# Stationary operands at byte 64, moving operands at byte 0 of each 128 bytes

## The chip, the cores and the metric

The kernel runs on one core of a Trainium2 chip. The core has TensorE (PE: matmuls; PEld: its weight loads), VectorE (DVE), ScalarE (ACT), GpSimd (POOL) and SyncE (SP, which only issues DMAs here), with SBUF and PSUM as on-chip memories of 128 partitions. The metric is the device time of one execution in microseconds (us); lower is better. Before the change three runs gave 1592.0 us as median (1591.66 to 1597.04).

## The reference

Two transformer blocks run one after the other on 256 tokens of width 1024, each two layers deep, all in float32.

```python
# first block, per layer: x and ctx are 256 tokens each; ctx is updated in layer 0 alone
sh1, sc1, gt1, sh2, sc2, gt2 = split(silu(c) @ w_ada + b_ada, 6)     # and the same for ctx
px = (rms_norm(x, g1) * (1 + sc1) + sh1) @ w_in
mix = concat([attention(q, k, v), fourier_mix(f), spatial_gate(u, gv)]) @ w_out
x = x + gt1 * mix
x = x + gt2 * (square(relu(modulate(rms_norm(x, g2)) @ w1)) @ w2)    # w1: 1024 x 4096
# second block, per layer
proj = rms_norm(x, g) @ w_in                                         # 1024 x 3656
x = x + concat([moba(...), diff_attention(...), sparse_attention(...)]) @ w_out
x = x + (silu(h @ w_gate) * (h @ w_up)) @ w_down                     # 1024 x 2816 and back
```

Nearly all the arithmetic is in the products with the large weights.

## The kernel before

**Three products for one.** A product of two float32 matrices is made of three matmuls of the type fp32r. Each operand is split into a high part and the rest, and hi x hi, hi x lo and lo x hi are summed in PSUM (`three`, line 2218; its matmul is line 2220). A matmul has a *stationary* operand (128 columns, loaded into the array by a LDWEIGHTS) and a *moving* one, which streams through. The load for the next matmul runs beside the stream of the present one. In the trace a matmul reads `output<-moving,stationary`.

**Which operand is which.** Where rows of tokens are the output (`rows1`, `rows2`, `down`), the activations are stationary (`act_hi`, `act_lo`, `hid1_*`, `hid2_*`, 128 tokens each) and 512 columns of weights move (256 or 328 in two blocks of the second `w_in`). Where columns are the output (`up1`, `up2`), 128 columns of weights are stationary and 512 tokens move in layer 0 of the first block, 256 tokens elsewhere. The opening of the first `up1` (`up1_open`) takes the two streams apart and so moves 256.

**Where weights come from.** SP loads 512 KB pieces into a ring of eight slots, `raw`; ScalarE writes the high part to `w_hi` (line 1175), VectorE the rest to `w_lo` (line 1581); TensorE multiplies, which frees the slot. `raw_of`, `hi_of` and `lo_of` give a piece's place; each slot has 32 floats (128 bytes) more than it needs, and `begins` (line 644) says at which float in the slot the piece starts: 16 (byte 64) for the kind "narrow", 0 for others. "narrow" are the up-products' weights with 256 moving columns, of `up1` in layer 1 and of `up2`.

**Where activations come from.** The norms and the mixing stages write `act_hi` on ScalarE and `act_lo` on VectorE. The same two tensors are stationary in `rows1`, `rows2` and `down` (through `act_of`) and moving in `up1`, `up2`.

**Order.** Every engine's program is written out by hand: `program` walks through the stages, and the tables FILL, FILL2 and OUT2 name the steps that are put between the weight pieces: turns (transposes on TensorE: data stationary, the identity moving), scores, values, modulation products. Buffers of stages that are not alive together share addresses, each following on the one before it, so a tensor's byte modulo 128 follows from the sizes ahead of it; `pad` shifts it.

Of the kernel before, what the change touches and what calls it, by code (L numbers as in the profile page):

```python
# [14 lines left out]
P = 128  # L15
# [87 lines left out]
def build(nc, A, consts, out, n):  # L103
    top = ExitStack()
    with top:
# [10 lines left out]
        act_hi = sb("act_hi", [P, KT, 2 * NT], F32R)  # L116
        act_lo = sb("act_lo", [P, KT, 2 * NT], F32R)
# [28 lines left out]
        with ExitStack() as s:  # L146
            cond_raw = sb("cond_raw", [P, KT, 2], F32, s)
            cond = sb("cond", [P, KT, 32], F32, s)
            mod = sb("mod", [P, 48, 2], F32, s)
# [3 lines left out]
            gains1 = sb("gains1", [P, DEPTH, 2 * DH + 256], F32, s)  # L153
            w_sp = sb("w_sp", [P, 4, P], F32, s)
            b_sp = sb("b_sp", [P, DEPTH, 4], F32, s)
            pad("pad_b_sp", 96, s)
            mod_rows = sb("mod_rows", [P, 2, W], F32, s)
            gate_b = sb("gate_b", [P, 2, D], F32, s)
# [4 lines left out]
            with ExitStack() as s2:  # L163
                proj1 = sb("proj1", [P, 2 * TT, IN1], F32, s2)
                q_t = sb("q_t", [P, NQ1 // 2, 2 * NT], F32, s2)
                k_t = sb("k_t", [P, NKV1, 2 * NT], F32, s2)
                four = sb("four", [P, 2, 2 * NT], F32, s2)
                w_sp_t = sb("w_sp_t", [P, 4, P], F32, s2)
                gtmp = sb("gtmp", [P, TT, 512], F32, s2)
# [4 lines left out]
                with ExitStack() as s3:  # L174
                    kdup = sb("kdup", [P, 2 * TT, 2 * NKV1, DH], F32, s3)
                with ExitStack() as s3:
                    probs1 = sb("probs1", [P, 2, 2, 2 * NT], F32, s3)
                    probs_t1 = sb("probs_t1", [P, 2, 2, 2 * TT, P], F32, s3)
# [4 lines left out]
            with ExitStack() as s2:  # L183
                xn1 = sb("xn1", [P, 2 * TT, D], F32, s2)
                below_wide = sb("below_wide", [P, 2 * TT, D], F32, s2)
                wide = sb("wide", [P, 4, NT], F32, s2)
        with ExitStack() as s:
# [5 lines left out]
            with ExitStack() as s2:  # L193
                proj2 = sb("proj2", [P, TT, IN2], F32, s2)
                pad("pad_proj2", 64, s2)
                pairs_t = sb("pairs_t", [P, 21, NT], F32, s2)
                ikdup = sb("ikdup", [P, TT, 2, DH], F32, s2)
                seen = sb("seen", [P, TT, NT], BF16, s2)
                relu_t = sb("relu_t", [P, 2, 2 * NT], F32, s2)
                score = sb("score", [P, TT, NT], F32, s2)  # L200
                diff_rows = sb("diff_rows", [P, TT, 4 * P], F32, s2)
                lam_in = diff_rows[:, :, 0:4 * DH]
# [3 lines left out]
                rope_a2 = sb("rope_a2", [P, 2, 512], F32, s2)  # L206
                probs2 = sb("probs2", [P, 2, 2, NT], F32, s2)
                probs_t2 = sb("probs_t2", [P, 4, 2 * TT, P], F32, s2)
            with ExitStack() as s2:
                hid2_hi = sb("hid2_hi", [P, FF2 // P, NT], F32R, s2)  # L210
                hid2_lo = sb("hid2_lo", [P, FF2 // P, NT], F32R, s2)
                fa2 = sb("fa2", [P, 2, 2 * NT], F32, s2)
                fb2 = sb("fb2", [P, 2, 2 * NT], F32, s2)
                xn_beside = sb("xn_beside", [P, TT, D], F32, s2)
            with ExitStack() as s2:
                xn2 = sb("xn2", [P, TT, D], F32, s2)
# [427 lines left out]
        def begins(i):  # L644

            return 16 if i < len(n.slots) and n.slots[i][0] == "narrow" else 0
# [221 lines left out]
        class Sync(Phases):  # L868
# [66 lines left out]
            def up1(self, l, h):  # L935
# [19 lines left out]
            def up2(self, l):  # L955
                for j in range(FF2 // 256):
                    for w in ("w_gate_2", "w_up_2"):
                        src = A[w][l].rearrange("(k p) n -> p k n", p=P)
                        for q in range(2):
                            self.put("narrow", 1024, lambda r: [(tiles(r, 4), src[:, 4 * q:4 * q + 4, j * 256:(j + 1) * 256])])  # L960
# [195 lines left out]
        class Scalar(Splitting):  # L1156
# [61 lines left out]
            def norm_part(self, m, which, streams, k0, k1):  # L1218
# [3 lines left out]
                for k in range(k0, k1):  # L1222
# [7 lines left out]
                    for s in streams:  # L1230
                        wait_wide(self.e, m, s, k)
                        nc.scalar.copy(act_hi[:, k, s * NT:(s + 1) * NT], wide_at(m, s, k)).then_inc(norm_hi, 1)
                        n.put("norm_hi", (m, s, k))

            def context_part(self, m, which, k0, k1):

                for k in range(k0, k1, 2):
# [8 lines left out]
                    nc.scalar.copy(act_hi[:, k:k + 2, 0:NT], wide[:, k % 4:k % 4 + 2, :]).then_inc(norm_hi, 1)  # L1246
# [16 lines left out]
            def norm_high(self, m, t, a):  # L1263
                self.e.wait_ge(xn_turned, n.at("xn_turned", (m, t, a)))
                nc.scalar.copy(act_hi[:, 4 * a:4 * a + 4, NT + t * P:NT + (t + 1) * P], tiles(turned_bank(m, t, a)[:], 4)).then_inc(norm_hi, 1)
# [132 lines left out]
            def out_(self, st, j):  # L1398
# [4 lines left out]
                nc.scalar.copy(act_hi[:, k:k + 2, c:c + NT], tiles(bank[b][:], 2)).then_inc(mix_hi, 1)  # L1403
# [50 lines left out]
            def diff_turn(self, l, t):  # L1454
                self.e.wait_ge(mix_full, n.at("mix_full", ("diff", l, t)))
                nc.scalar.mul(act_hi[:, 2 + 2 * t:4 + 2 * t, 0:NT], tiles(bank[7][:], 2), sub_g[:, l:l + 1]).then_inc(mix_hi, 1)
# [113 lines left out]
        class Vector(Splitting):  # L1570
# [90 lines left out]
            def context_part(self, m, k0, k1, row=None):  # L1661
# [4 lines left out]
                def low(k):  # L1666
                    e.wait_ge(norm_hi, n.at("norm_hi", (m, CTX, k + 1)))
                    nc.vector.tensor_tensor(act_lo[:, k:k + 2, 0:NT], wide[:, k % 4:k % 4 + 2, :], act_hi[:, k:k + 2, 0:NT].bitcast(F32),
# [17 lines left out]
            def norm_part(self, m, streams, k0, k1):  # L1686
# [4 lines left out]
                def low(k):  # L1691
                    for s in streams:
                        e.wait_ge(norm_hi, n.at("norm_hi", (m, s, k)))
                        nc.vector.tensor_tensor(act_lo[:, k, s * NT:(s + 1) * NT], wide_at(m, s, k),
                                                act_hi[:, k, s * NT:(s + 1) * NT].bitcast(F32), ALU.subtract).then_inc(norm_lo, 1)
# [46 lines left out]
            def norm_low(self, m, t, a):  # L1742
                self.e.wait_ge(norm_hi, n.at("norm_hi", (m, t, a)))
                at_ = slice(4 * a, 4 * a + 4), slice(NT + t * P, NT + (t + 1) * P)
                nc.vector.tensor_tensor(act_lo[:, at_[0], at_[1]], tiles(turned_bank(m, t, a)[:], 4), act_hi[:, at_[0], at_[1]].bitcast(F32),  # L1745
# [180 lines left out]
            def mix_low(self, key, b, k, c):  # L1926
                self.e.wait_ge(mix_hi, n.at("mix_hi", key))
                nc.vector.tensor_tensor(act_lo[:, k:k + 2, c:c + NT], tiles(b, 2), act_hi[:, k:k + 2, c:c + NT].bitcast(F32),
# [149 lines left out]
            def diff_turn(self, l, t):  # L2078
                self.e.wait_ge(mix_hi, n.at("mix_hi", ("diff", l, t)))
                c = slice(2 + 2 * t, 4 + 2 * t)  # L2080
                nc.vector.scalar_tensor_tensor(act_lo[:, c, 0:NT], tiles(bank[7][:], 2), sub_g[:, l:l + 1], act_hi[:, c, 0:NT].bitcast(F32),
# [135 lines left out]
        class Tensor(Phases):  # L2217
# [141 lines left out]
            def act_of(self, k, g):  # L2359
                return [a[:, k, g * P:(g + 1) * P] for a in (act_hi, act_lo)]  # L2360
# [333 lines left out]
            def up1_open(self):  # L2694

                e, m, first = self.e, 1, self.i
                for s in (CTX, X):
                    for j in range(2):
# [3 lines left out]
                        for q in range(2):  # L2702
# [9 lines left out]
                            for kk, f in ((kk, f) for kk in range(4) for f in range(2)):  # L2712
                                k, idx = 4 * q + kk, 2 * j + f
                                if j == f == 0:
                                    e.wait_ge(norm_lo, n.at("norm_lo", (m, s, k)))
                                ins = self.three(up1_bank(0, 0, idx)[:, s * NT:(s + 1) * NT], [v[:, kk, f * P:(f + 1) * P] for v in w],
                                                 [a[:, k, s * NT:(s + 1) * NT] for a in (act_hi, act_lo)], (s, k) == (CTX, 0))
# [6 lines left out]
            def up1(self, l, h):  # L2724
# [8 lines left out]
                for j in range(opened, FF1 // 256 // HALVES[l]):  # L2733
                    for q in range(2):
# [4 lines left out]
                        for f in range(2):  # L2739
# [6 lines left out]
                            for kk in range(4):  # L2746
# [3 lines left out]
                                ins = self.three(o, [v[:, kk, f * P:(f + 1) * P] for v in w], [a[:, k, c0:2 * NT] for a in (act_hi, act_lo)],  # L2750
# [140 lines left out]
```

## Time and profile before

| | |
|---|---|
| median of three runs | 1592.0 us |
| profiled execution | 1594.35 us, span 1592.6 us |
| TensorE busy | 97% of the span, 9164 matmul records |
| weight loads | 79% |
| VectorE, ScalarE, GpSimd | 65%, 50%, 7% |
| DMA | 202 GB/s on average, 322 MB |

The span is the time from the first to the last instruction of the profiled execution. Matmuls overlap: a record with 512 columns lasts some 392 ns, but the next one starts before it ends, so busy time says little and the distance between starts says much. A float32 matmul that isn't a turn has two records, a three-product matmul and a turn have one. The up-products of the second block (1076 to 1196 us and 1409 to 1528 us) are the "narrow" ones. The trace is of one execution, and line numbers are those of the kernel before.

### The profile page before, as it was taken

How to read it: one execution, taken by the hardware profiler on the slowest of the kernel's cores; microseconds unless marked ns; L12 is line 12 of the kernel's file. 1: busy time of each engine (PE TensorE's matmuls, PEld its weight loads, DVE VectorE, ACT ScalarE, POOL GpSimd, SP SyncE). 2: the span in 40 equal slices, each digit the busy share in tenths (PEclk: the TensorE clock that was granted, in tenths of full speed). 3: DMA queues.
4: the chain of work that ended last, by engine and by line, in shares of the span. 5: the costliest groups of instructions: out<-in, count | busy, mean ns of one | idle time of the engine just before them, and what ended most of it. 6: DMA issues, size and time to landing. Idle time of an engine off the chain costs nothing.

```text
span 1592.6 us, 23486 instructions
## 1 busy us (share of the span) xinstructions
PE 1541.2 (97%) x9164; PEld 1262.6 (79%) x9164; DVE 1028.4 (65%) x1577; ACT 795.5 (50%) x1356; POOL 114.2 (7%) x130
## 2 busy tenths in 40 slices
PE   6999999999999999998999999999999999999999
PEld 2864689778888887567898878779998787689987
DVE  3637756455456437576785576978995558879973
ACT  3537735343345225565664456645554456555542
POOL 0111000010001000100000031010000111000000
PEclk9999999999999999999999999999999999999999
DMA  9528623487568524586998689436665596356653
GB/s 360 152 84 313 215 75 114 145 264 253 162 220 277 162 66 133 176 279 190 335 319 300 211 272 312 160 108 183 191 197 191 184 326 227 106 141 192 198 190 115
DMA packets 201005, 322.41 MB, mean 202 GB/s; under 512 B 14576, under 2 KB 100864, under 8 KB 200768
## 3 DMA queue, kind: packets, MB, share of 16 engines
q1 hardware_dynamic: 192992, 293.51, 57.6%
q0 software_dynamic: 7680, 27.34, 4.8%
q8 instruction: 73, 1.20, 0.3%
q14 instruction: 36, 0.29, 0.1%
q10 hardware_dynamic: 224, 0.07, 0.0%
HBM read 298.27 MB, written 22.61 MB: 201 GB/s over the span
## 4 chain that ended last, share of the span: by engine, by line
PE 86%; DVE 7%; DMA 3%; ACT 2%; issue 1%; POOL 0%; SPq 0%; POOLq 0%; DVEq 0%; ACTq 0%
PE bank L2220 53%; PE pair_bank L2220 21%; PE bank L2289 2%; DVE w_lo L1581 1%; PE bank L2537 1%; PE pair_bank L2506 1%; DMA raw<-in_w_in 1%; PE bank L2517 1%; DMA raw<-in_w_ada 1%; PE bank L2315 1%; PE pair_bank L2557 1%; DMA raw<-in_w_mlp 1%; PE bank L2425 0%; PE bank L2571 0%; ACT w_hi L1175 0%
## 5 line engine op out<-in xcount | busy, mean ns | idle before, releaser
L1581 DVE TENSOR_TENSOR w_lo<-raw,w_hi 128x1024 fp32r<-128x1024 f32 (+2 forms) x374 | 447.4, 1218 | 273.5 <-ACT w_hi L1175 272.0
L1175 ACT CAST w_hi<-raw 128x1024 fp32r<-128x1024 f32 (+1 forms) x416 | 428.4, 1045 | 363.2 <-PE bank L2220 236.6
L2220 PE MATMUL pair_bank<-act_hi,w_hi 128*128 128x256 f32 (+1 forms) x744 | 226.8, 305 | 5.0 <-DVE act_lo L1745 2.1
L2220 PE MATMUL pair_bank<-act_hi,w_lo 128*128 128x256 f32 (+1 forms) x744 | 224.7, 302 | 0.0
L2220 PE MATMUL pair_bank<-act_lo,w_hi 128*128 128x256 f32 (+1 forms) x744 | 224.6, 302 | 0.0
L2220 PE MATMUL bank<-w_hi,hid_hi 128*128 128x512 f32 x560 | 220.2, 393 | 0.0
L2220 PE MATMUL bank<-w_lo,hid_hi 128*128 128x512 f32 x560 | 219.6, 392 | 0.0
L2220 PE MATMUL bank<-w_hi,hid_lo 128*128 128x512 f32 x560 | 219.4, 392 | 0.0
L2220 PE MATMUL bank<-w_hi,act_hi 128*128 128x512 f32 (+2 forms) x528 | 206.6, 391 | 8.4 <-DVE w_lo L1581 4.0
L2220 PE MATMUL bank<-w_hi,act_lo 128*128 128x512 f32 (+2 forms) x528 | 200.3, 379 | 0.0
L2220 PE MATMUL bank<-w_lo,act_hi 128*128 128x512 f32 (+2 forms) x528 | 200.1, 379 | 0.0
L2220 PEld LDWEIGHTS pair_bank<-act_hi,w_hi 128*128 128x128 f32 x744 | 140.9, 189 | 16.6 <-issue 6.4
L2220 PE MATMUL bank<-act_hi,w_hi 128*128 128x256 f32 (+1 forms) x504 | 148.7, 295 | 0.9 <-DVE w_lo L1581 0.9
L2220 PE MATMUL bank<-act_hi,w_lo 128*128 128x256 f32 (+1 forms) x504 | 147.9, 293 | 0.0
L2220 PE MATMUL bank<-act_lo,w_hi 128*128 128x256 f32 (+1 forms) x504 | 147.8, 293 | 0.0
L2220 PEld LDWEIGHTS pair_bank<-act_lo,w_hi 128*128 128x128 f32 x744 | 140.8, 189 | 7.2 <-issue 0.7
L2220 PEld LDWEIGHTS pair_bank<-act_hi,w_lo 128*128 128x128 f32 x744 | 140.7, 189 | 6.3
L2220 PEld LDWEIGHTS bank<-w_hi,hid_hi 128*128 128x128 f32 x560 | 105.1, 188 | 23.9 <-issue 0.2
L2220 PEld LDWEIGHTS bank<-w_hi,hid_lo 128*128 128x128 f32 x560 | 105.1, 188 | 23.9
L2220 PEld LDWEIGHTS bank<-w_lo,hid_hi 128*128 128x128 f32 x560 | 105.2, 188 | 23.6 <-issue 0.2
L2220 PEld LDWEIGHTS bank<-w_hi,act_hi 128*128 128x128 f32 x528 | 100.0, 189 | 29.1 <-DVE w_lo L1581 5.3
L2220 PEld LDWEIGHTS bank<-w_hi,act_lo 128*128 128x128 f32 x528 | 99.9, 189 | 19.3
(249 smaller groups left out, 2088.9 us busy)
## 6 DMA issues: line engine op xcount, KB each, us to landing
raw<-in_w_mlp SPq DMA_DIRECT2D x128, 512.0 KB, 4.9
raw<-in_w_in SPq DMA_DIRECT2D x112, 512.0 KB, 4.5
raw<-in_w_ada SPq DMA_DIRECT2D x96, 512.0 KB, 5.6
raw<-in_w_gate SPq DMA_DIRECT2D x44, 512.0 KB, 3.8
raw<-in_w_up SPq DMA_DIRECT2D x44, 512.0 KB, 3.8
raw<-in_w_down SPq DMA_DIRECT2D x44, 512.0 KB, 3.6
split_lo<-w_lo POOLq DMA_DIRECT2D x36, 512.0 KB, 5.0
w_lo<-split_lo SPq DMA_DIRECT2D x36, 512.0 KB, 5.1
```

What stands on the lines that cost most here:

```text
L1175: nc.scalar.copy(hi_of(i)[:, 0:w], raw_of(i)[:, 0:w]).then_inc(hi_ready, 1)
L1581: nc.vector.tensor_tensor(lo_of(i)[:, 0:w], raw_of(i)[:, 0:w], hi_of(i)[:, 0:w].bitcast(F32), ALU.subtract).then_inc(lo_ready, 1)
L2220: ins = nc.tensor.matmul(o, a[x], b[y], start=first and i == 0, stop=True, skip_group_check=True)
L2289: ins = nc.tensor.matmul(bank[bk][j:j + 32, :], cond[:, k, :], tiles(raw[:, r, 0:1024], 2)[:, kk, :], start=k < 4, stop=True, skip_group_c ...
L2315: nc.tensor.matmul(bank[bk][:], sel_b[:, s, :], mod_rows[:, bk % 2, :], start=True, stop=True, skip_group_check=True).then_inc(ada_turned, 1)
L2506: nc.tensor.matmul(bank[a][:, 0:w], st["q"][a], st["k"][a], start=True, stop=True).then_inc(scored, 1)
L2517: ins = nc.tensor.matmul(st["o"][a], st["v"][a][kt], probs_t1[:, j % 2, a, kt, :], start=kt == 0, stop=kt == keys - 1)
L2537: ins = nc.tensor.transpose(bank[2 + a][:, kt * P:(kt + 1) * P], probs1[:, j % 2, a, kt * P:(kt + 1) * P], ident)
L2557: nc.tensor.matmul(bank[a][:, 0:w], st["q"][a], st["k"][a], start=True, stop=False)
```

## The change

The change moves operands within 128 bytes and does nothing else: instructions, their order and their waits are the same on every engine. Pads of 64 bytes are put into the SBUF allocation; the kind "narrow" is named "up" and now holds layer 0 of `up1` too; and `act_hi`, `act_lo` get rows of 512 + 32 floats with two views of the same memory, one that starts at byte 64 (index 0, for uses as stationary) and one at byte 0 (index 1, for uses as moving). Norms write the view that the next product reads (`m % 2` is 1 ahead of the up-products).

Bytes modulo 128 of the operands, from the allocation:

| matmuls | count | stationary, moving before | after |
|---|---|---|---|
| three products, 512 columns | 3840 | 0, 0 | 64, 0 |
| three products, 256 columns, `up1` layer 1 and `up2` | 2880 | 64, 0 | 64, 0 |
| three products, 256 columns, others (192 in `up1_open`) | 336 | 0, 0 | 64, 0 |
| three products, 328 columns | 96 | 0, and 0, 32 or 64 | 64, and 0, 32 or 64 |
| turns of activations, probabilities and modulation rows | 632 | 0 (40 at 32), 0 | 64 (40 at 96), 0 |
| scores and values of the first block | 208 | 0, 0 | 64, 0 |
| values of the second block with stationary `proj2` | 48 | 0 or 32, and 0 or 8 | 64 or 96, the same |
| modulation (`ada`) | 192 | 0, 0 | 64, 0 |
| scores and logits of the second block, mask products | 160 | 0, 0 | 0, 0 |
| values of the second block with moving `proj2` | 24 | 0, and 0 or 32 | 0, and 64 or 96 |
| Fourier, spatial and gate products | 54 | 0 or 8, and 0, 8 or 124 | 64 or 8, and 0, 8, 64 or 124 |

```diff
-        act_hi = sb("act_hi", [P, KT, 2 * NT], F32R)
-        act_lo = sb("act_lo", [P, KT, 2 * NT], F32R)
+        act_hi_room = sb("act_hi_room", [P, KT, 2 * NT + 32], F32R)
+        act_lo_room = sb("act_lo_room", [P, KT, 2 * NT + 32], F32R)
+
+        def act_views(room):
+            return [room[:, :, at_:at_ + 2 * NT] for at_ in (16, 0)]
+
+        act_hi, act_lo = act_views(act_hi_room), act_views(act_lo_room)
...
             cond_raw = sb("cond_raw", [P, KT, 2], F32, s)
+            pad("pad_cond", 64, s)
             cond = sb("cond", [P, KT, 32], F32, s)
+            pad("end_cond", 64, s)
...
+                pad("pad_proj1", 64, s2)
                 proj1 = sb("proj1", [P, 2 * TT, IN1], F32, s2)
                 q_t = sb("q_t", [P, NQ1 // 2, 2 * NT], F32, s2)
+                pad("end_q_t", 64, s2)
                 k_t = sb("k_t", [P, NKV1, 2 * NT], F32, s2)
...
+                pad("pad_hid1", 64, s2)
                 hid1_hi = sb("hid1_hi", [P, 16 * 2 * NT], F32R, s2)
                 hid1_lo = sb("hid1_lo", [P, 16 * 2 * NT], F32R, s2)
+                pad("pad_fa1", 64, s2)
...
+                pad("pad_hid2", 64, s2)
                 hid2_hi = sb("hid2_hi", [P, FF2 // P, NT], F32R, s2)
                 hid2_lo = sb("hid2_lo", [P, FF2 // P, NT], F32R, s2)
+                pad("pad_fa2", 64, s2)
...
-            return 16 if i < len(n.slots) and n.slots[i][0] == "narrow" else 0
+            return 16 if i < len(n.slots) and n.slots[i][0] == "up" else 0
...
-                        self.put("narrow" if l else "w", 1024, lambda r: [(tiles(r, 4), src[:, 4 * q:4 * q + 4, c:c + 256])])
+                        self.put("up", 1024, lambda r: [(tiles(r, 4), src[:, 4 * q:4 * q + 4, c:c + 256])])
...
-                        nc.scalar.copy(act_hi[:, k, s * NT:(s + 1) * NT], wide_at(m, s, k)).then_inc(norm_hi, 1)
+                        nc.scalar.copy(act_hi[m % 2][:, k, s * NT:(s + 1) * NT], wide_at(m, s, k)).then_inc(norm_hi, 1)
...
-                nc.scalar.copy(act_hi[:, k:k + 2, c:c + NT], tiles(b, 2)).then_inc(mix_hi, 1)
+                nc.scalar.copy(act_hi[0][:, k:k + 2, c:c + NT], tiles(b, 2)).then_inc(mix_hi, 1)
...
-                return [a[:, k, g * P:(g + 1) * P] for a in (act_hi, act_lo)]
+                return [a[:, k, g * P:(g + 1) * P] for a in (act_hi[0], act_lo[0])]
...
-                                ins = self.three(o, [v[:, kk, f * P:(f + 1) * P] for v in w], [a[:, k, c0:2 * NT] for a in (act_hi, act_lo)],
+                                ins = self.three(o, [v[:, kk, f * P:(f + 1) * P] for v in w], [a[:, k, c0:2 * NT] for a in (act_hi[1], act_lo[1])],
...
```

The lines left out are pads of the same kind (around `w_sp`, `mod_rows`, `w_sp_t`, `kdup`, `probs1`, `xn1`, `wide`, `proj2`, `ikdup`, `diff_rows`, `probs2`, `xn_beside`, `xn2`) and the same two indices at the other places that write or read `act_hi` and `act_lo`.

## Rows read from the trace of the kernel before

**Rows 1.** The page, parts 1 and 2: the span, busy times, TensorE's clock.

```profile
span 1592.6 us, 23486 instructions
...
PE 1541.2 (97%) x9164; PEld 1262.6 (79%) x9164; DVE 1028.4 (65%) x1577; ACT 795.5 (50%) x1356; POOL 114.2 (7%) x130
...
PEclk9999999999999999999999999999999999999999
```

**Rows 2.** TensorE's waits: who waited for whom, us in total, times, longest.

```profile
PE bank L2289 <- DMA raw<-in_w_ada: 5.1, 1, 5.1
...
PE bank L2220 <- DVE w_lo L1581: 4.8, 5, 2.1
```

**Rows 3.** Windows, line 2220 alone: stretch, length, PE busy (starts), clock, DMA share, GB/s.

```profile
45.40:98.60 53.20, 52.57 (x228) 1.00 0.39 112
192.00:229.00 37.00, 37.00 (x162) 1.00 0.19 58
262.40:335.40 73.00, 68.55 (x290) 1.00 0.52 168
336.00:604.00 268.00, 266.31 (x1152) 1.00 0.59 193
703.00:725.00 22.00, 21.95 (x95) 1.00 0.64 199
832.90:920.90 88.00, 88.00 (x385) 1.00 0.77 250
1196.00:1256.50 60.50, 60.50 (x265) 1.00 0.57 178
1528.50:1589.00 60.50, 60.50 (x265) 1.00 0.43 141
```

**Rows 4.** Chain that ended last: start us, length us, engine, output, line, matmuls.

```profile
237.92 5.76 PE pair_bank L2220 x48
...
1076.17 11.24 PE pair_bank L2220 x96
1087.40 10.88 PE bank L2220 x96
```

**Rows 5.** Windows, line 2220 alone, three short stretches.

```profile
381.44:387.79 6.35, 6.35 (x29) 1.00 0.35 90
429.68:435.29 5.61, 5.61 (x25) 1.00 0.52 180
1076.10:1079.70 3.60, 3.53 (x30) 1.00 0.33 119
```

**Rows 6.** TensorE's timeline, 328 columns: seventh and tenth matmul after a turn.

```profile
962.58 0.31 PE L2220 MATMUL bank<-w_hi,act_hi 128*128 128x328 f32 x1
...
963.03 0.31 PE L2220 MATMUL bank<-w_hi,act_hi 128*128 128x328 f32 x1
```

**Rows 7.** Chain that ended last: turns of both blocks.

```profile
44.96 0.44 PE pair_bank L2338 x4
...
961.41 0.44 PE bank L2425 x4
```

**Rows 8.** Windows, all engines: length, busy us (instructions) each, clock, DMA share, GB/s.

```profile
104.00:188.00 84.00, 80.41 (x596) 44.43 (x594) 57.54 (x155) 61.75 (x163) 7.98 (x5) 0.96 0.73 260
216.00:600.00 384.00, 384.00 (x1789) 313.70 (x1788) 197.69 (x244) 150.38 (x205) 20.20 (x37) 1.00 0.54 176
1073.00:1187.00 114.00, 112.24 (x988) 111.79 (x987) 103.27 (x85) 59.07 (x73) 0.59 (x1) 1.00 0.64 186
```

**Rows 9.** The page, part 5: the split of the weights; us busy, mean ns.

```profile
L1581 DVE TENSOR_TENSOR w_lo<-raw,w_hi 128x1024 fp32r<-128x1024 f32 (+2 forms) x374 | 447.4, 1218 | 273.5 <-ACT w_hi L1175 272.0
L1175 ACT CAST w_hi<-raw 128x1024 fp32r<-128x1024 f32 (+1 forms) x416 | 428.4, 1045 | 363.2 <-PE bank L2220 236.6
```

**Rows 10.** Windows, all engines, projections of the second block, both layers.

```profile
924.00:1019.00 95.00, 92.12 (x486) 71.99 (x485) 67.85 (x162) 57.04 (x127) 22.75 (x19) 1.00 0.84 277
1282.00:1320.00 38.00, 38.00 (x210) 31.45 (x209) 20.95 (x55) 24.21 (x59) 5.68 (x4) 1.00 0.97 320
```

More of the change, by code:

```diff
@@ L153, in build @@
             gains1 = sb("gains1", [P, DEPTH, 2 * DH + 256], F32, s)
+            pad("pad_w_sp", 64, s)
             w_sp = sb("w_sp", [P, 4, P], F32, s)
@@ L157, in build @@
             mod_rows = sb("mod_rows", [P, 2, W], F32, s)
+            pad("end_mod_rows", 64, s)
             gate_b = sb("gate_b", [P, 2, D], F32, s)
@@ L163, in build @@
             with ExitStack() as s2:
+                pad("pad_proj1", 64, s2)
                 proj1 = sb("proj1", [P, 2 * TT, IN1], F32, s2)
                 q_t = sb("q_t", [P, NQ1 // 2, 2 * NT], F32, s2)
+                pad("end_q_t", 64, s2)
                 k_t = sb("k_t", [P, NKV1, 2 * NT], F32, s2)
                 four = sb("four", [P, 2, 2 * NT], F32, s2)
+                pad("pad_w_sp_t", 64, s2)
                 w_sp_t = sb("w_sp_t", [P, 4, P], F32, s2)
+                pad("end_w_sp_t", 64, s2)
                 gtmp = sb("gtmp", [P, TT, 512], F32, s2)
@@ L174, in build @@
                 with ExitStack() as s3:
+                    pad("pad_kdup", 64, s3)
                     kdup = sb("kdup", [P, 2 * TT, 2 * NKV1, DH], F32, s3)
                 with ExitStack() as s3:
+                    pad("pad_probs1", 64, s3)
                     probs1 = sb("probs1", [P, 2, 2, 2 * NT], F32, s3)
+                    pad("end_probs1", 64, s3)
                     probs_t1 = sb("probs_t1", [P, 2, 2, 2 * TT, P], F32, s3)
             with ExitStack() as s2:
+                pad("pad_hid1", 64, s2)
                 hid1_hi = sb("hid1_hi", [P, 16 * 2 * NT], F32R, s2)
                 hid1_lo = sb("hid1_lo", [P, 16 * 2 * NT], F32R, s2)
+                pad("pad_fa1", 64, s2)
                 fa1 = sb("fa1", [P, 2, 2 * NT], F32, s2)
             with ExitStack() as s2:
+                pad("pad_xn1", 64, s2)
                 xn1 = sb("xn1", [P, 2 * TT, D], F32, s2)
                 below_wide = sb("below_wide", [P, 2 * TT, D], F32, s2)
+                pad("pad_wide", 64, s2)
                 wide = sb("wide", [P, 4, NT], F32, s2)
@@ L193, in build @@
             with ExitStack() as s2:
+                pad("pad_proj2", 64, s2)
                 proj2 = sb("proj2", [P, TT, IN2], F32, s2)
-                pad("pad_proj2", 64, s2)
                 pairs_t = sb("pairs_t", [P, 21, NT], F32, s2)
+                pad("pad_ikdup", 64, s2)
                 ikdup = sb("ikdup", [P, TT, 2, DH], F32, s2)
+                pad("end_ikdup", 64, s2)
                 seen = sb("seen", [P, TT, NT], BF16, s2)
@@ L200, in build @@
                 score = sb("score", [P, TT, NT], F32, s2)
+                pad("pad_diff_rows", 64, s2)
                 diff_rows = sb("diff_rows", [P, TT, 4 * P], F32, s2)
+                pad("end_diff_rows", 64, s2)
                 lam_in = diff_rows[:, :, 0:4 * DH]
@@ L206, in build @@
                 rope_a2 = sb("rope_a2", [P, 2, 512], F32, s2)
+                pad("pad_probs2", 64, s2)
                 probs2 = sb("probs2", [P, 2, 2, NT], F32, s2)
+                pad("end_probs2", 64, s2)
                 probs_t2 = sb("probs_t2", [P, 4, 2 * TT, P], F32, s2)
             with ExitStack() as s2:
+                pad("pad_hid2", 64, s2)
                 hid2_hi = sb("hid2_hi", [P, FF2 // P, NT], F32R, s2)
                 hid2_lo = sb("hid2_lo", [P, FF2 // P, NT], F32R, s2)
+                pad("pad_fa2", 64, s2)
                 fa2 = sb("fa2", [P, 2, 2 * NT], F32, s2)
                 fb2 = sb("fb2", [P, 2, 2 * NT], F32, s2)
+                pad("pad_xn_beside", 64, s2)
                 xn_beside = sb("xn_beside", [P, TT, D], F32, s2)
             with ExitStack() as s2:
+                pad("pad_xn2", 64, s2)
                 xn2 = sb("xn2", [P, TT, D], F32, s2)
@@ L2716, in up1_open @@
                                 ins = self.three(up1_bank(0, 0, idx)[:, s * NT:(s + 1) * NT], [v[:, kk, f * P:(f + 1) * P] for v in w],
-                                                 [a[:, k, s * NT:(s + 1) * NT] for a in (act_hi, act_lo)], (s, k) == (CTX, 0))
+                                                 [a[:, k, s * NT:(s + 1) * NT] for a in (act_hi[1], act_lo[1])], (s, k) == (CTX, 0))
                                 if s == X and k == KT - 1 and f == 0:
@@ L2848, in up2 @@
                                     ins = self.three(b[:, f * NT:(f + 1) * NT], [v[:, kk, f * P:(f + 1) * P] for v in w],
-                                                     [a[:, k, NT:2 * NT] for a in (act_hi, act_lo)], k == 0 and f == 0)
+                                                     [a[:, k, NT:2 * NT] for a in (act_hi[1], act_lo[1])], k == 0 and f == 0)
                             self.took(ins, ("up2", l, j, which) if q == 1 else None)
```

22 lines of the change are left out of this document (11 added, 11 removed).

## The prediction

> **What bounds the kernel now.** I read the page's first two parts first. TensorE is busy for 97% of the span, VectorE for 65%, and TensorE's clock is granted at 9 tenths or more in every slice [rows 1]. Then the waits of TensorE: the longest is the first load, and those for the split of the weights come to 4.8 us in five waits [rows 2]. So nearly everything that ends late is TensorE's own work. Then I asked the windows and the chain of waits for the *pace*: they give a time and a count of back-to-back matmuls, and time over count is the distance from one matmul's start to the next. That distance, not the duration of one matmul (which overlaps its successor), is what the end of the kernel is made of. Of the three-product matmuls 3840 have 512 moving columns, 3216 have 256 and 96 have 328. In eight stretches 2842 of the 512-column ones keep TensorE busy for 655.4 us, 230.6 ns each [rows 3]: 41% of the span in one kind of instruction. DMA moves 58 to 250 GB/s there. The other 998 or so stand in short groups between turns, scores and values.
>
> **What the placement does to the pace.** The kernel already holds both placements for one shape. The opening products of the first MLP have 256 columns with stationary and moving both at byte 0: 48 in 5.76 us, 120.0 ns each. The later up-products have 256 columns too, with the stationary at byte 64: 96 in 10.88 us, 113.3 ns each [rows 4]. The difference is 6.7 ns. What a column costs comes from two shapes in the same placement: the steadiest 512-column stretch has 29 starts, 28 intervals, in 6.35 us, 226.7 ns [rows 5] against 120.0 for 256, so 0.417 ns per column, one column per cycle at 2.4 GHz, the level that the clock share of 1.00 in those rows means. The fixed part is then 120.0 - 106.7 = 13.3 ns with both at byte 0, and 6.7 ns with the stationary at 64. If it depends on the length as little with 64 as it does with 0, a settled 512-column matmul takes 213.3 + 6.7 = 220.0 ns.
>
> Two things speak for caution. First, 64 alone doesn't give the low pace: it settles. The first 96 of a run of up-products take 11.24 us, the next 96 take 10.88 [rows 4], and the first 30 go by in 3.53 us, 118 ns each [rows 5]. Second, the 328-column products read moving operands at bytes 0, 32 and 64 in turn against a stationary at byte 0. Those at 64, which lie as far apart as the change wants it, take 0.45 us for three, 150 ns [rows 6]; 328 x 0.417 + 13.3 is 150.0. They gain nothing. They are groups of three, so they may never settle; or longer products don't profit at all. That is the main doubt.
>
> **The change part by part.**
> - *Long runs of 512 columns.* 2842 x (230.6 - 220.0) = 30.1 us. Until a run settles it stays near its old pace. Modulation and gate products cut the eight stretches into some 15 runs; 15 x 12 matmuls x 10 ns = 1.8 us less, so 28.3 us. Bounds: at the top, all of the fixed part goes, 2842 x (230.6 - 213.3) = 49 us; at the bottom, the pace becomes that of the worst steady stretch of today, 24 intervals in 5.61 us, 233.8 ns [rows 5], which loses 2842 x 3.2 = 9 us. I take 220.0, as the nearest shape (same operands, same loads) shows it.
> - *Short groups of 512, and 328.* About 1000 and 96 matmuls, mostly in groups of 9 to 24 that are cut by turns. By the 328s they gain nothing; by the unsettled up-products, 118 against 120, 2 ns each, 2 us in all. I take 1 us. At the bottom they lose the same 3.2 ns, 3 us.
> - *Opening products.* 192 of 256 columns go from 120.0 to 113.3: 1.3 us; with settling I take 1.0.
> - *Turns.* Their stationary moves from byte 0 (in one tensor every other one at 32) to 64 (96). Four take 0.44 us, 110 ns each, whether all stand at byte 0 (line 2338) or two at 0 and two at 32 (line 2425, second block) [rows 7]. So I take 0; if the 632 of them moved as the products do, by 6.7 ns, it would be 4 us either way, mostly where TensorE waits in any case.
> - *Scores, values and modulation.* In the attention of the first layer, 596 matmul records, weights are being loaded for only 44 of 84 us, and ScalarE is busy for 62 and VectorE for 58 [rows 8]: loads lie much less beside streams there. I take 0; the bound by 6.7 ns a record is 4 us either way, and as much for the two layers' other attention stretches together.
> - *VectorE, ScalarE, DMA.* Instructions, order and waits are the same; only addresses differ. What hides their work is TensorE's pace: in the two-row stages 512 KB of weights feed 12 matmuls, 2.77 us now, 2.64 afterwards. The split of such a piece takes 1.05 us on ScalarE and 1.22 us on VectorE [rows 9], so both stay below. The loads rise from 178 to some 187 GB/s in the last stage and from 250 to 262 in the fullest of rows 3, which is below what the projections of the second block draw, 277 and 320 GB/s [rows 10]. If that cover went, a stretch would fall back to its loads; only those projections are near it, and I book 0.5 us lost there.
>
> Sum: 28.3 + 1 + 1 - 0.5 = 30 us. The profiled execution took 1594.35 us (span 1592.6 and 1.75 around it), so 1564.4 for one like it; the median of the runs shown is 2.35 us below it, so 1562.
>
> The Trainium skill has a rule against this: SBUF — State Buffer, table of the section "A bandwidth-pool intuition that's wrong (but worth ruling out)", gives TensorE a second independent read port for loading weights, beside that for the moving operand. By that the placement is nothing and the time stays 1592. The 120.0 against 113.3 ns of one shape does not fit the rule; the 328 columns do [rows 4, 6]. Its page TensorE: Matmul & The Clock Gate, section "Back-to-back issue gap", gives N/2.4 + 2.5 ns for a warm matmul, 215.8 ns for 512 columns; the stretches of rows 3 are 15 ns above it, and by it the first term would be 42 us.
>
> **Rivals.**
> 1. *Longer products don't profit* (no change, 1591). In the up stage TensorE is loading weights for 111.8 of 114 us; in the first layer's MLP, nearly all of 512 columns, for 314 of 384 [rows 8]. So a load that is disturbed less shortens the first, and in the second it has time to spare. For it: the 328 columns. Against it: the fixed part is 13.3 ns at 256, 328 and 512 columns alike with both at 0, as if one cause made it. Only the opening products gain then, 1 us.
> 2. *It settles halfway* (1580). 226.7 ns is a steady state that exists today [rows 5]. If 64 only makes all long runs reach it, the term is 2842 x 3.9 = 11 us, and 1 for the rest: 1592 - 12.
> 3. *It settles wrongly* (slower, 1602). The same kernel has steady stretches at 233.8 ns with its operands at byte 0 like all others [rows 5], so the place within 128 bytes isn't all that counts. If the pairs at 64 fall into that state in the long runs, it costs 9 us, and 1 in the short groups. It decides from a pace above 230.6.
> 4. *More than I booked* (about 1548): the fixed part falls to half of 6.7 ns, 9.5 us more, and the short groups settle too, 1000 x 5 ns.
>
> **How the numbers follow.** My forecast, long runs settled near 220 ns, has a chance of 0.50 and by itself a range of 1555 to 1573 (settling in a few or in many matmuls). Rival 1: 0.17. Rival 2: 0.16. Rival 3: 0.09. Rival 4: 0.08. A difference under 0.5%, 8 us, can't be told from none here. So faster: 0.50 + 0.16 + 0.08 = 0.74; same: rival 1 and a little of rival 3, 0.18; slower: 0.08. The range, 1552 to 1591, takes in rivals 1 and 2 and leaves out rival 3 and most of rival 4.
>
> **What would show it.** The two windows of 60.5 us with 265 matmuls shrink to 58, the 88 us with 385 to 84.5. The opening 48 take 5.5 us. The up-products keep 113.3 ns and four turns 0.44 us. TensorE's waits stay within a few us. If the 512-column pace is 230 with the rest as said, rival 1 is right; 226.7 or 234 would be rivals 2 and 3. If the pace is 220 and the end is still near 1590, the time went back to loads, which would stand in TensorE's waits as w_lo or raw.

## The result, and the profile after

The changed kernel takes 1604.0 us (median of four runs, 1602.6 to 1608.6) against 1592.3 for the kernel before beside it: a ratio of 1.0065, with a 95% interval of 1.0049 to 1.0081. It is slower by 0.65%, and the interval leaves out 1. The forecast was 1562 (1552 to 1591). The profiled execution took 1603.83 us, 9.5 more than that of before. Among all the runs below one stands apart and is left out of the ratios: of e5's six executions one took 3070.7 us, the others 1600.0 to 1602.4.

The page of the kernel after, parts 1 and 2, answers to [rows 1]:

```profile
span 1602.0 us, 23486 instructions
...
PE 1553.4 (97%) x9164; PEld 1272.4 (79%) x9164; DVE 1029.5 (64%) x1577; ACT 795.4 (50%) x1356; POOL 113.5 (7%) x130
...
PEclk8999999999999999999999999999999999999999
```

The same instructions ran, and VectorE, ScalarE and GpSimd were as busy as before. TensorE is busy for 12.2 us longer. In the first 40 us its granted clock is 0.87 of full speed after and 0.91 before; in all the windows below it is 1.00 in both. Its waits, the two of [rows 2] again (who waited for whom, us in total, times, longest):

```profile
PE bank L2319 <- DMA raw<-in_w_ada: 5.1, 1, 5.1
PE bank L2250 <- DVE w_lo L1611: 4.6, 4, 2.1
```

They are nearly what they were (5.1 and 4.8). So the time went into the distance between matmuls. Windows of the kernel after over the three-product line (2250 now) alone, in the columns of [rows 3]: stretch, length, PE busy (records), PEld busy (records), clock, DMA share, GB/s.

```profile
262.40:335.20 72.80, 68.35 (x289) 53.77 (x288) 1.00 0.52 168
335.90:424.90 89.00, 88.97 (x384) 72.16 (x384) 1.00 0.70 231
...
834.30:922.90 88.60, 88.60 (x385) 71.98 (x384) 1.00 0.76 249
...
1081.00:1191.00 110.00, 110.00 (x942) 110.00 (x941) 1.00 0.64 187
1201.20:1261.80 60.60, 60.60 (x265) 49.38 (x264) 1.00 0.56 177
...
1421.00:1531.00 110.00, 110.00 (x942) 110.00 (x941) 1.00 0.65 188
1537.80:1598.40 60.60, 60.60 (x265) 49.38 (x264) 1.00 0.43 140
```

The 512-column stretches are nearly where they were: the two of 265 take 60.60 us for 60.50, the one of 385 takes 88.60 for 88.00 [rows 3]. The new thing stands in the two windows of 110 us, which lie inside the up stages of the second block, 256 columns. Inside the same stages the kernel before has, with the same columns:

```profile
1080.00:1190.00 110.00, 110.00 (x973) 110.00 (x972) 1.00 0.66 193
...
1415.00:1525.00 110.00, 110.00 (x973) 110.00 (x972) 1.00 0.66 193
```

973 records fitted into 110 us, and now 942 do. (A count takes in two or three matmuls that began ahead of the window; by the distance of starts it is 113.3 ns before and 117.1 now.) The chain of waits shows it from the stage's first matmul on (start us, length us, engine, output, line, matmuls), against 11.24 and then 10.88 for 96 in [rows 4]; ahead of it stand the first opening products, 5.76 before, and four turns, 0.44 in [rows 7]:

```profile
44.78 0.44 PE pair_bank L2368 x4
...
238.30 5.60 PE pair_bank L2250 x48
...
1077.51 11.46 PE pair_bank L2250 x96
1088.97 11.24 PE bank L2250 x96
1100.21 11.24 PE pair_bank L2250 x96
```

The run of up-products never comes down to the low pace: it stays at 11.24 for 96, 117.1 ns each, where it had gone down to 10.88. The whole stages, 1056 products each, grow from 119.6 to 123.5 and 123.6 us, 7.9 us together; the up stage of the first block's layer 1 has 692 records in the 88 us from 739 on where it had 700, about 1 us. That is 8.9 of the 9.5 us. The opening products give back 0.16 us in the first 48 and 0.4 in all four groups; the eight 512-column stretches of [rows 3] lose 1.7 together, from first start to last; what lies between them gains about 0.7.

Yet the change leaves the up-products' bytes modulo 128 alone (64 and 0, before and after). What it alters for them is the *row* of their moving operand: a row of `act_hi` and `act_lo` was 2048 bytes and is now 2176, so that two k-tiles (blocks of 128 rows of the product's inner dimension) lie 2176 apart, and the low half lies 17408 bytes behind the high one in place of 16384.

### The profile page after: what moved, and what is told of

The parts are those of the page before. It is cut to its first block, busy times and chain, and to the rows that moved or that the text cites. A ratio compares the mean times of both kernels' runs of the same rounds, so it can differ in the third digit from the quotient of the medians.

```text
span 1602.0 us, 23486 instructions
## 1 busy us (share of the span) xinstructions
PE 1553.4 (97%) x9164; PEld 1272.4 (79%) x9164; DVE 1029.5 (64%) x1577; ACT 795.4 (50%) x1356; POOL 113.5 (7%) x130
## 4 chain that ended last, share of the span: by engine, by line
PE 86%; DVE 7%; DMA 2%; ACT 2%; issue 2%; POOL 0%; SPq 0%; POOLq 0%; DVEq 0%; ACTq 0%
PE bank L2250 53%; PE pair_bank L2250 21%; PE bank L2319 2%; DVE w_lo L1611 1%; PE bank L2567 1%; PE pair_bank L2536 1%; PE bank L2547 1%; DMA raw<-in_w_in 1%; PE bank L2345 1%; PE pair_bank L2587 1%; DMA raw<-in_w_ada 1%; DMA raw<-in_w_mlp 1%; PE bank L2455 0%; PE bank L2601 0%; ACT w_hi L1205 0%
## 5 line engine op out<-in xcount | busy, mean ns | idle before, releaser
L2250 PE MATMUL pair_bank<-act_hi_room,w_hi 128*128 128x256 f32 (+1 forms) x744 | 228.4, 307 | 3.8 <-DVE act_lo_room L1775 2.1
L2250 PE MATMUL pair_bank<-act_lo_room,w_hi 128*128 128x256 f32 (+1 forms) x744 | 226.2, 304 | 0.0
L2250 PE MATMUL pair_bank<-act_hi_room,w_lo 128*128 128x256 f32 (+1 forms) x744 | 225.9, 304 | 0.0
L2250 PE MATMUL bank<-w_hi,act_hi_room 128*128 128x512 f32 (+2 forms) x528 | 207.2, 393 | 7.5 <-DVE w_lo L1611 4.0
L2250 PE MATMUL bank<-w_hi,act_lo_room 128*128 128x512 f32 (+2 forms) x528 | 201.1, 381 | 0.0
L2250 PE MATMUL bank<-w_lo,act_hi_room 128*128 128x512 f32 (+2 forms) x528 | 200.5, 380 | 0.0
L2250 PEld LDWEIGHTS pair_bank<-act_hi_room,w_hi 128*128 128x128 f32 x744 | 140.8, 189 | 15.1 <-issue 6.0
L2250 PE MATMUL bank<-act_hi_room,w_hi 128*128 128x256 f32 (+1 forms) x504 | 150.0, 298 | 0.6 <-DVE w_lo L1611 0.6
L2250 PE MATMUL bank<-act_lo_room,w_hi 128*128 128x256 f32 (+1 forms) x504 | 149.1, 296 | 0.0
L2250 PE MATMUL bank<-act_hi_room,w_lo 128*128 128x256 f32 (+1 forms) x504 | 148.9, 295 | 0.0
L2250 PEld LDWEIGHTS bank<-w_hi,act_hi_room 128*128 128x128 f32 x528 | 100.1, 190 | 28.3 <-DVE w_lo L1611 5.3
```

The source lines that it names most:

```text
L2250: ins = nc.tensor.matmul(o, a[x], b[y], start=first and i == 0, stop=True, skip_group_check=True)
```

## The experiments

*Distance* below is the start of the stationary operand minus that of the moving one, in bytes modulo 256. *Pace* is the mean distance of successive starts, in the kernels of their own over the second half of a stretch.

### Which part of the change costs the time

Theory "row step": the up-products' 113.3 ns needs the moving rows to step by a multiple of 256 bytes. Rivals: the distance of the two halves ("low half"), or anything else in the change ("elsewhere"). The kernel before with the longer rows alone, the kernel after with the old rows, and the kernel after with rows of 2304 bytes:

```diff
# e1_rows2176, in the kernel before
-        act_hi = sb("act_hi", [P, KT, 2 * NT], F32R)
-        act_lo = sb("act_lo", [P, KT, 2 * NT], F32R)
+        act_hi_room = sb("act_hi_room", [P, KT, 2 * NT + 32], F32R)
+        act_lo_room = sb("act_lo_room", [P, KT, 2 * NT + 32], F32R)
+        act_hi, act_lo = act_hi_room[:, :, 0:2 * NT], act_lo_room[:, :, 0:2 * NT]
# e2_after_rows2048, in the kernel after (act_lo_room alike)
-        act_hi_room = sb("act_hi_room", [P, KT, 2 * NT + 32], F32R)
+        act_hi_room = sb("act_hi_room", [P, KT, 2 * NT], F32R)
-            return [room[:, :, at_:at_ + 2 * NT] for at_ in (16, 0)]
+            return [room[:, :, at_:at_ + 2 * NT] for at_ in (0, 0)]
# e3_after_rows2304, in the kernel after (act_lo_room alike)
-        act_hi_room = sb("act_hi_room", [P, KT, 2 * NT + 32], F32R)
+        act_hi_room = sb("act_hi_room", [P, KT, 2 * NT + 64], F32R)
```

Expected of the first:

> The kernel before, with nothing but the rows of act_hi and act_lo lengthened from 2048 to 2176 bytes (views still at byte 0 of the room, slots, pads and hidden tensors as before). 'Row step' and 'low half': up2 falls from 113.3 to 117 ns, the stage of 119.7 us takes 123.5, the kernel 1600 to 1606 us. 'Elsewhere': 1591 to 1594 us.

Of the second:

> The kernel after, with the rows of act_hi and act_lo back at 2048 bytes and both views at byte 0; everything else of the change stays. 'Row step' and 'low half': up2 back at 113.3 ns and 119.7 us, the kernel 1591 to 1595 us. 'Elsewhere': 1602 to 1606 us.

Of the third:

> The kernel after, with rows of 2304 bytes in place of 2176 (the views stay at byte 64 and byte 0). 'Row step' with a modulus of 256 bytes: up2 back at 113.3 ns, the kernel 1591 to 1595 us. 'Row step' with a larger modulus (512 and more), or 'low half' (18432 apart now), or 'elsewhere': 117 ns and 1602 to 1606 us.

Measured, beside 1594.2 us for the kernel before on that chip: e1 1603.6, ratio 1.0047 (1.0029 to 1.0066); e2 1595.5, 1.0001 (0.9986 to 1.0017); e3 1595.8, 1.0015 (0.9998 to 1.0032). One 110 us window in the first of the two up stages of e1, e2 and e3, three-product line alone:

```profile
1081.00:1191.00 110.00, 110.00 (x942) 110.00 (x941) 1.00 0.65 187
```

```profile
1078.00:1188.00 110.00, 110.00 (x973) 110.00 (x972) 1.00 0.66 193
```

```profile
1081.00:1191.00 110.00, 110.00 (x973) 110.00 (x972) 1.00 0.66 194
```

The longer row alone makes the kernel before slow, and taking it away, or giving it 128 bytes more, brings the 973 records back. "Elsewhere" falls; "low half" stands badly, since e3 moves the low half further still (18432). e2 and e3 end 0.5 and 0.8 us above the range that was expected of them, on a chip on which the kernel before took 1594.2. e3 says one thing more: it is the whole change with another row length, and it comes to nothing, 0.15% with an interval of -0.02% to 0.32%. (e2 takes back more than the rows: the stationary views of the two tensors start at byte 0 again.)

### The placements by themselves

A kernel without anything beside the products shows the paces one by one.

```python
# m1_places: one stretch; chain() yields byte places as the up-products walk them
for st, mv, b, first in chain(256, 96, sa=64, ma=1152, pitch=2048, apart=16384, slot=4224):
    nc.tensor.matmul(bank[b][:, 0:256], arena[:, st:st + P], arena[:, mv:mv + 256], start=first, stop=True, ...)
```

> A kernel of its own that leaves the whole computation out: 38 stretches of chained three-product sequences from one SBUF array, 288 products of 256 columns or 144 of 512 (180 of 384) each, two products of 512 and four of 64 columns between stretches; only the byte places differ. Stretch 1 has the places of the up-products of before (weights at byte 64 mod 128, slots 4224 bytes apart, moving rows 2048 bytes apart, low half 16384 bytes behind the high one), stretch 2 those of after (rows 2176 apart, low half 17408 behind). Theory 'row step' (the settled pace needs the moving row to keep its place modulo 256 bytes from one k to the next): stretch 1 at 113.3 ns, 2 and 3 (2176 apart) at 116 to 118, 4 (2048 apart, only the low half moved by 1024) at 113.3, 5 to 7 (2304, 2560, 3072 apart) at 113.3, 8 and 9 (2112, 2080 apart) above 115. Rival 'low half' (the distance of the two halves decides): 4 at 116 to 118 and 3 at 113.3. Rival 'elsewhere' (not the moving operand at all): 1 to 9 alike. Weights' start (stretches 10 to 16): 64 at 113.3, 0 at 119 to 120 if the opening products' pace comes from the place. 512 columns (stretches 26 to 36): 229 to 233 at every place if the placement in 128 bytes does not matter to them; one of them at 220 if the change only missed the right place.

Windows of m1_places over TensorE's matmuls, 15 us each, in the second half of stretches 1, 2, 4, 5, 8, 10 and 33: stretch, length, PE busy (records), clock, DMA share, GB/s.

```profile
64.00:79.00 15.00, 15.00 (x135) 1.00 0.00 1
99.00:114.00 15.00, 15.00 (x131) 1.00 0.00 1
168.00:183.00 15.00, 15.00 (x135) 1.00 0.00 1
201.00:216.00 15.00, 15.00 (x135) 1.00 0.00 1
302.00:317.00 15.00, 15.00 (x130) 1.00 0.00 1
372.00:387.00 15.00, 15.00 (x128) 1.00 0.00 1
...
1168.00:1183.00 15.00, 15.00 (x68) 1.00 0.00 1
```

| 256 columns, weights at byte 64, slots 4224 apart | pace, ns |
|---|---|
| rows 2048 apart, low half 16384 or 17408 behind | 113.3, 113.3 |
| rows 2176 apart, low half 17408 or 18432 behind | 116.3, 116.3 |
| rows 2304, 2560, 3072 apart | 113.3, 113.3, 113.3 |
| rows 2112, 2080 apart | 117.8, 118.0 |
| rows 2048 apart, weights at byte 0, 16, 32, 48, 80, 96, 112 | 117.7 to 118.9 |
| rows 2048 apart, moving rows at byte 32, 64, 64 of 128 | 118.8 to 119.0 |

"Row step" holds and "low half" falls: 17408 costs nothing with rows of 2048. (All distances of the halves tried here are multiples of 256 bytes.) For 256 columns the place within 128 bytes does matter, too: of the starts in the table only 64 against 0 settles at 113.3, and it does so only while the rows step by multiples of 256. Weights at byte 0, expected at 119 to 120, had 118.9. With DMA near zero in all rows the other engines have no part in it. Of 512 columns one stretch was low, the one whose distance is 0 throughout (226.7; the last row above). That led to the next one.

> A kernel of its own as m1_places, again without the computation: 58 stretches of 192 products of 256 columns or 96 of 512 (144 of 328). Now all weight slots lie a multiple of 256 bytes apart, so that the distance from the moving operand's start to the stationary one's keeps one value modulo 256 in a stretch. Stretches 1 to 16: 512 columns at distances 0, 16, ... 240; 17 to 32: 256 columns at the same distances; 33 to 50: one of the low halves (weights' or rows') moved by 64, 128 or 192 against its high half; 51 to 54: 328 columns at distances 0, 64, 128, 192. Theory 'distance' (the pace hangs on the distance of the two operands modulo 256 bytes): 256 columns at 113.3 ns for 64 and 118 to 120 for 0, 128 and 192; 512 columns at 226.7 for 0 and 229 to 234 elsewhere (m1_places had 226.7 in its stretch 33, the only one with distance 0 throughout). Rival 'length decides' (a longer product has its own overhead whatever the distance): 512 columns within 1 ns of one value at all sixteen. If one of the sixteen is at 220, the forecast of 220 had the wrong place and not the wrong idea.

Windows of m2_distances at 512 columns, distances 0, 32 and 128, then at 256 columns, distances 0, 64, 128 and 192:

```profile
53.00:68.00 15.00, 15.00 (x68) 1.00 0.00 1
99.00:114.00 15.00, 15.00 (x66) 1.00 0.00 0
...
238.00:253.00 15.00, 15.00 (x67) 1.00 0.00 0
...
426.00:441.00 15.00, 15.00 (x127) 1.00 0.01 1
520.00:535.00 15.00, 15.00 (x129) 1.00 0.00 1
613.00:628.00 15.00, 15.00 (x129) 1.00 0.00 1
708.00:723.00 15.00, 15.00 (x135) 1.00 0.01 1
```

At 512 columns: 226.7 ns at distance 0, 233.3 at 64, 232.4 at 128, 228.9 at 192, 228.3 to 234.3 at the twelve others; with one low half moved against its high half, 228.9 to 233.3. None is at 220. At 328 columns all four distances lie at 150.0 to 151.7. "Length decides" falls, since the sixteen distances differ by up to 7.6 ns; "distance" holds for 512. It missed at 256: distance 64 was expected at 113.3 and had 117.8, while 192, expected at 118 to 120, had 113.3. m1_places had it the other way round with the same two distances (slots 4096 apart). Either the place counts beyond 256 bytes, or one placement has two paces. With the low half of the moving operand 64, 128 or 192 bytes off a multiple of 256 behind the high one, 256 columns took 117.8 to 119.3 ns, in one stretch each.

> A kernel of its own, again without the computation: six placements, each in eight stretches that differ only in 0 to 7 extra short products (64 + 8 e columns) ahead of them: 256 columns at distance 64 and at distance 192, slots 4096 bytes apart (stretches 1 to 8, 9 to 16), the same with slots 4352 apart (17 to 24, 25 to 32), 512 columns at distance 0 and 128, slots 4096 apart (33 to 40, 41 to 48). Theory 'entry' (a placement allows several steady paces, and how a stretch is entered picks one): at 256 columns both 113.3 and some 118 ns turn up within at least one group of eight. Rival 'place alone': all eight of a group alike in their second half, 113.3 in stretches 1 to 8 and 25 to 32, 117.8 in 9 to 24, 226.7 in 33 to 40, 232.4 in 41 to 48, as one stretch of each showed before.

Windows of m3_entries, in the second half of its first eight stretches, all at 256 columns and distance 64, which differ only in what ran ahead of them:

```profile
53.00:68.00 15.00, 15.00 (x134) 1.00 0.01 1
76.00:91.00 15.00, 15.00 (x129) 1.00 0.01 1
99.00:114.00 15.00, 15.00 (x135) 1.00 0.00 1
122.00:137.00 15.00, 15.00 (x130) 1.00 0.01 1
146.00:161.00 15.00, 15.00 (x130) 1.00 0.00 1
170.00:185.00 15.00, 15.00 (x135) 1.00 0.00 1
194.00:209.00 15.00, 15.00 (x130) 1.00 0.00 1
218.00:233.00 15.00, 15.00 (x135) 1.00 0.00 1
```

Four of eight go at 113.3, four at 117.8, and nothing between; at distance 192 it is two and six. With slots 4352 apart the same entries give the same paces, so nothing beyond 256 bytes counts here. "Entry" holds: at 256 columns a constant distance of 64 or 192 has two steady paces. At 512 columns the entry hardly matters: eight of eight at 226.7 for distance 0, seven at 232.4 and one at 233.3 for 128.

Why did the kernel before settle? Its slots lie 4224 bytes apart, which swaps 64 and 192 from slot to slot, every 24 products. The five stretches of m1_places and m2_distances with such slots, rows of 2048 and a start at 64 against 0 were all at 113.3 in their second half. With rows 2176 apart the moving operand swaps the distance every three products, and none of eight such runs came down (three each in the kernel after and in e1, two in m1_places). It is not the number of swaps, though. High and low weights lie in rings of five and eight slots, so in part of the slots the low third has the other distance (192, 192, 64), and the distance changes at two products of three; the first 96 products in the window of m1_places' stretch 1 above are of this kind, and they go at 113.3 like the rest, as such slots do, where no wait is among them, in layer 1 of the first block in the kernel before. Two stretches of m2_distances have both cases by themselves, the low half of the weights 128 bytes off (64, 64, 192) and the low half of the moving operand 128 bytes off (64, 192, 64); 10 us of their second halves:

```profile
1085.00:1095.00 10.00, 10.00 (x91) 1.00 0.00 0
...
1155.00:1165.00 10.00, 10.00 (x87) 1.00 0.01 2
```

The first goes at 113.3, the second, entered in one way only, at 117.8. So a swap between 64 and 192 that comes from the weights does not keep a run from 113.3, and one that comes from the moving operand was not seen at 113.3 in any run here.

### What this is worth in the kernel

If the distance decides, the 3840 products of 512 columns can be moved both ways without the change. In the kernel before 2040 of them lie at distance 0 and 1800 at 128, since odd slots begin 128 bytes further modulo 256. The edit begins the wide pieces of the odd slots (e4) or of the even ones (e5) 128 bytes later and moves `hid2` by 128 (`raw_of`, `hi_of` and `lo_of` hand in the slot's number `r`; not shown):

```diff
-        def begins(i):
-            return 16 if i < len(n.slots) and n.slots[i][0] == "narrow" else 0
+        def begins(i, r):
+            kind = n.slots[i][0] if i < len(n.slots) else "w"
+            return {"narrow": 16, "ada": 0}.get(kind, 32 if r % 2 else 0)      # e5: 0 if r % 2 else 32
...
+                pad("pad_hid2", 128, s2)
                 hid2_hi = sb("hid2_hi", [P, FF2 // P, NT], F32R, s2)
```

> The kernel before with one edit: wide weights begin at byte 128 of the odd ring slots and at byte 0 of the even ones, and hid2 lies 128 bytes later, so that the starts of the two operands of all 3840 products of 512 columns lie 0 apart modulo 256 (before: 2040 at 0, 1800 at 128). The up-products' slots and rows are as before. 'Distance': these products go from some 230.6 to 226.7 ns, the value of m2_distances at distance 0, in stretches of more than a few dozen; 3840 x 3.9 = 15 us at most, less where a stretch is short or settles late: 1577 to 1585 us, mlp2's 264 products in 59.8 us in place of 60.5; up2 stays at 113.3 ns. 'Length decides' or 'settles by chance': 1591 to 1595 us.

> The same edit the other way round: byte 128 in the even slots, 0 in the odd ones, hid2 moved alike, so that all 3840 products of 512 columns have distance 128. 'Distance': 232.4 ns, the value of m2_distances at distance 128, in place of 230.6: 3840 x 1.8 = 7 us, 1597 to 1602 us. 'Length decides' or 'settles by chance': 1591 to 1595 us, as e4.

Measured beside 1594.6 us for the kernel before: e4 1583.5, ratio 0.9926 (0.9910 to 0.9942); e5 1602.2, ratio 1.0044 (1.0028 to 1.0060). Windows of e4, three-product line alone: the two middle stages of the first MLP, the last product of layer 1 in the first block, an up stage, the two last products of the second block:

```profile
333.20:420.40 87.20, 87.20 (x384) 71.98 (x385) 1.00 0.72 236
420.60:507.40 86.80, 86.80 (x384) 71.88 (x383) 1.00 0.70 238
...
825.10:911.90 86.80, 86.80 (x385) 71.87 (x384) 1.00 0.76 256
1072.00:1182.00 110.00, 110.00 (x973) 110.00 (x972) 1.00 0.66 194
1188.00:1247.70 59.70, 59.70 (x266) 49.39 (x264) 1.00 0.57 181
...
1518.90:1578.40 59.50, 59.50 (x264) 49.26 (x264) 1.00 0.44 143
```

The same of e5:

```profile
336.20:425.50 89.30, 89.30 (x383) 72.25 (x384) 1.00 0.69 230
425.80:515.10 89.30, 89.30 (x384) 71.85 (x383) 1.00 0.68 232
...
839.60:928.60 89.00, 89.00 (x385) 72.20 (x385) 1.00 0.76 247
1087.00:1197.00 110.00, 110.00 (x973) 110.00 (x972) 1.00 0.67 195
1202.60:1263.50 60.90, 60.90 (x264) 49.38 (x263) 1.00 0.55 176
...
1536.00:1597.00 61.00, 61.00 (x264) 49.47 (x263) 1.00 0.41 139
```

Both operands start at byte 0 of 128 in both kernels, the up-products are alike (973), and the times lie 18.7 us apart; e5 ends 0.2 us above its expected range. In the traces the mean pace of back-to-back 512-column products is 227.3 ns in e4 and 232.6 in e5, against 226.7 and 232.4 alone. The same mean is 230.5 in the kernel before, so these products account for 3840 x 3.2 = 12 us in e4 and 3840 x 2.1 = 8 us in e5; measured are 11.0 gained and 7.7 lost. The other 336 products of 256 columns and the 96 of 328, whose weights move along, account for some 1.5 us at most. The two last products, 60.50 us each in [rows 3], take 59.7 and 59.5 in e4, 60.9 and 61.0 in e5. e4 is faster than both kernels, by 0.74% than before. That the distance counts and not the weights' own place, which is all that differs between e4 and e5, can be read from the trace of before and the allocated addresses: beside `hid1`, which lies at 128 modulo 256, weights at 128 go at 228.6 ns and weights at 0 at 232.1; beside `hid2`, which lies at 0, it is the other way round, 232.6 and 228.0.

## Why the prediction was wrong

- *What bounds the kernel, and the pace as its measure.* Right: no wait moved, and what changed is the distance between starts.
- *Long runs of 512 columns, the step that failed.* The term of 28.3 us rested on "if it depends on the length as little with 64 as it does with 0, a settled 512-column matmul takes 213.3 + 6.7 = 220.0 ns". It does depend on the length. At distance 0 the fixed part is 13.3 ns at 256 and at 512 columns (120.0 and 226.7, m2_distances), as the prediction took it from rows 4 and 5. At 64 it is 6.7 or 11.1 ns at 256 columns, and 20.0 at 512 (15.6 at 192). By the allocated addresses, the 512s of the kernel after lie at distances 64 and 192, with mean paces of 231.7 and 230.7 in its trace; those of before at 0 and 128, with 228.9 and 232.4. Weighted by their numbers that is 231.2 against 230.5: a good and a bad half were traded for two middling ones, and the term came out a little below zero: 1.7 us lost in the eight stretches. What I had read as one pace of 230.6 in [rows 3] was a mixture of two, which the ring's slot pitch made. In [rows 5] the two parts stand side by side: the stretch at 226.7 has distance 0 throughout, the one at 233.8 has 128 in two products of three. Splitting the starts by distance modulo 256 would have shown it in the trace of before.
- *"The up-products keep 113.3", the other step that failed.* This alone makes the kernel slower. I looked at bytes modulo 128, in which their places do not change, and gave the new row length of the moving operand no price; the section on the change even says that operands move within 128 bytes and nothing else is done. It is 8.9 us for 2880 products, some 3 ns each (e1: 1603.6 us with this alone; e2 and e3: none of it). Of the 39.4 us between the 1564.4 that were added up for a profiled execution and the 1603.8 measured, 30 are the long runs (28.3 booked, 1.7 lost) and 8.9 the up-products.
- *Opening products.* 1.0 us booked; 5.76 to 5.60 us for the first 48, 0.4 us over the four groups. The sign was right; they read the long rows too and got as far as 117, as those do.
- *Short groups and 328 columns.* 1 us booked; the 328s gained nothing, as m2_distances shows for every distance. The seventh and the tenth after a turn, as in [rows 6], start 0.44 us apart in the timeline of after:

```profile
963.81 0.31 PE L2250 MATMUL bank<-w_hi,act_hi_room 128*128 128x328 f32 x1
...
964.25 0.31 PE L2250 MATMUL bank<-w_hi,act_hi_room 128*128 128x328 f32 x1
```

- *Turns, scores, values, modulation at nothing.* Right for the turns, 0.44 us for four as before. No run takes the others by themselves; the whole change with rows of 2304 bytes, e3, is at 1595.8 us, ratio 1.0015.
- *The rivals.* Rival 1 ("longer products don't profit") forecast the 512s' pace, 230, but for a wrong reason and with a time, 1591, that missed the loss elsewhere. Its reason was that a load beside a longer product has time to spare; then the distance would not matter to 512 columns, and e4 and e5 show that it does. Rival 2 had 226.7 as what 64 gives; 226.7 exists, at distance 0. Rival 3 had the time, 1602, by luck: it booked a loss of 9 us in the long 512-column runs, which lost 1.7, and it was the 256s that went into a worse state.

In the prediction I set the Trainium skill's rule of a second, independent read port for weight loads (SBUF — State Buffer, section "A bandwidth-pool intuition that's wrong (but worth ruling out)") against the 120.0 and 113.3 ns of one shape. e4 and e5 speak against it for this kernel: if loads and streams were read without regard to each other, the distance between the two operands should not be worth 18.7 us. Where the two meet no run shows.

What stays open: why two steady paces exist at 256 columns and what in the entry picks one, why a moving operand that changes its place modulo 256 from product to product keeps the run from the low pace when weights that do the same do not, and why of all distances 0 is good for 512 columns and bad for 256. No run looks inside.

## What to carry to other kernels

When matmuls stand back to back, group their starts by the distance of the two operands' addresses (modulo 256 bytes here) before taking a mean pace for a property of the shape: a mean may hide a good and a bad half. A pad that aligns one operand can also lengthen a row, so list for every other reader of that tensor where its rows now start (here a step of 2048 or 2304 bytes was harmless and one of 2176 cost 8.9 us). And a pace seen at one length is not to be carried to another by its fixed part alone: at 256 and at 512 columns different placements were best.

## What the hardware showed that I had not expected

- Byte places of the two operands alone moved a 512-column fp32r product between 226.7 and 234.3 ns and a 256-column one between 113.3 and 120.7, at a granted clock of 1.00 and with next to no DMA beside them.
- One placement can have two steady paces, 113.3 and 117.8 ns, with nothing but a few short products ahead of the run to choose between them, and both last to the end of a stretch of 192.
- The best places for 256 columns (distances 64 and 192, 113.3 ns at best against 120.0 at 0) are not the best for 512 (226.7 ns at distance 0 against 233.3 at 64 and 228.9 at 192).
- For the low pace at 256 columns the rows of the moving operand had to step by a multiple of 256 bytes (2048, 2304, 2560, 3072); at 2176, 2112 and 2080 it was 116.3 to 118.0 ns.
